# A two-layer transformer block with a state-space block behind it: products read the unscaled residual, and the branch ends work in column quarters

## The reference

```python
def rms_norm(x, g):
    y = xf * lax.rsqrt(jnp.mean(xf * xf, axis=-1, keepdims=True) + EPS)
    return (y * g.astype(jnp.float32)).astype(x.dtype)

for l in range(DEPTH):                       # DEPTH = 2
    xn = rms_norm(h, mix_pre_g[l])
    proj = jnp.einsum('bsd,dc->bsc', xn, w_in[l])      # q, k, v, latents, gates of three mixers
    ...
    h = h + rms_norm(jnp.einsum('bsc,cd->bsd', mix, w_out[l]), mix_post_g[l])
    xa = memory_attention(rms_norm(h, x_pre_g[l]), rms_norm(mem, mem_g[l]), x_wq[l], x_wkv[l], x_wo[l])
    h = h + rms_norm(xa, x_post_g[l])
    ff = swiglu(rms_norm(h, f_pre_g[l]), f_w_gu[l], f_w_down[l])
    h = h + rms_norm(ff, f_post_g[l])
# then second_block: rms_norm, one wide projection, sliding-window attention, an SSM, a GLU
```

## Time and profile before

| | us |
|---|---|
| median of 3 runs (lowest, highest) | 3474.57 (3471.28, 3475.05) |
| span of the profiled execution | 3474.8 |
| PE busy | 3189.5 (92%) |
| DVE busy | 2075.9 (60%) |
| ACT busy | 1525.5 (44%) |
| POOL busy | 166.6 (5%) |

### The profile page before, as it was taken

One profiled execution on the slowest core, in us unless ns is written; L12 is line 12 of the kernel. 1 busy time (PEld: TensorE's weight loads), 2 busy tenths in 40 slices (PEclk: granted clock), 3 DMA queues, 4 the chain that ended last, 5 costly groups with the idle time before them and its releaser, 6 DMA issues.

```text
span 3474.8 us, 48434 instructions
## 1 busy us (share of the span) xinstructions
PE 3189.5 (92%) x17364; PEld 2765.8 (80%) x17364; DVE 2075.9 (60%) x2251; ACT 1525.5 (44%) x1942; POOL 166.6 (5%) x131
## 2 busy tenths in 40 slices
PE   7898897899999997998978999999998977888999
PEld 6798776688888886987866888888876876778997
DVE  5466755555555555577646555555556568987554
ACT  5454544443444344545444443444444443334443
POOL 0000000000000000000000000000001012221000
PEclk9999998899999998999988999999998998889999
DMA  6554453555555554544634555555554333333555
GB/s 235 175 178 165 146 187 109 177 187 188 187 187 189 189 184 134 194 152 140 206 109 154 191 186 190 188 183 191 188 174 136 131 101 107 116 119 129 187 177 176
DMA packets 158218, 577.15 MB, mean 166 GB/s; under 512 B 17409, under 2 KB 20145, under 8 KB 156401
## 3 DMA queue, kind: packets, MB, share of 16 engines
q1 hardware_dynamic: 151120, 549.52, 48.3%
q10 hardware_dynamic: 4800, 13.51, 1.1%
q0 software_dynamic: 2144, 12.02, 1.0%
HBM read 568.43 MB, written 6.55 MB: 165 GB/s over the span
## 4 chain that ended last, share of the span: by engine, by line
PE 76%; DVE 10%; issue 4%; ACT 4%; DVEq 4%; POOL 1%; ACTq 1%; POOLq 0%; DMA 0%
PE acc L600 19%; PE acc L602 19%; PE acc L601 19%; PE acc L608 5%; PE acc L610 5%; PE acc L611 5%; PE tp L619 2%; DVE lo L1359 2%; DVE sr L1880 1%; ACT hi L944 1%; DVEq L1890 1%; POOL small L1962 1%; ACT lg L997 1%; DVE sd L1887 1%; PE tp L900 1%
## 5 line engine op out<-in xcount | busy, mean ns | idle before, releaser
L1359 DVE TENSOR_TENSOR lo<-raw,hi 128x1024 fp32r<-128x1024 f32 x1040 | 1271.8, 1229 | 1017.0 <-ACT hi L944 1008.7
L944 ACT ACTIVATE hi<-raw 128x1024 fp32r<-128x1024 f32 x1040 | 1095.5, 1058 | 1350.0 <-PE acc L602 1005.3
L600 PE MATMUL acc<-hi,xh 128*128 128x512 f32 (+2 forms) x2272 | 883.7, 389 | 0.0
L602 PE MATMUL acc<-hi,xl 128*128 128x512 f32 (+2 forms) x2272 | 876.2, 386 | 0.0
L601 PE MATMUL acc<-lo,xh 128*128 128x512 f32 (+2 forms) x2272 | 876.1, 386 | 0.0
L608 PE MATMUL acc<-xh,hi 128*128 128x256 f32 x1664 | 494.9, 297 | 56.3 <-DVE lo L1359 56.2
L600 PEld LDWEIGHTS acc<-hi,xh 128*128 128x128 f32 x2272 | 429.4, 189 | 85.6 <-issue 1.3
L602 PEld LDWEIGHTS acc<-hi,xl 128*128 128x128 f32 x2272 | 428.8, 189 | 85.1
L601 PEld LDWEIGHTS acc<-lo,xh 128*128 128x128 f32 x2272 | 429.3, 189 | 82.9
L610 PE MATMUL acc<-xl,hi 128*128 128x256 f32 x1664 | 484.1, 291 | 0.0
L611 PE MATMUL acc<-xh,lo 128*128 128x256 f32 x1664 | 483.8, 291 | 0.0
(11 more groups left out here) (347 smaller groups left out, 2832.9 us busy)
## 6 DMA issues: line engine op xcount, KB each, us to landing
raw<-in_stream SPq DMA_DIRECT2D x1040, 512.0 KB, 4.2
gpost<-in_post_g POOLq DMA_DIRECT2D x6, 1024.0 KB, 6.7
bpad<-in_b_pad ACTq DMA_DIRECT2D x8, 512.0 KB, 3.2
row<-in_rows POOLq DMA_DIRECT2D x3, 896.0 KB, 6.1
toep_scratch<-toep ACTq DMA_DIRECT2D x1, 2304.0 KB, 8.1
y<-in_mem SPq DMA_DIRECT2D x1, 2048.0 KB, 8.0
h<-in_x ACTq DMA_DIRECT2D x1, 2048.0 KB, 14.4
mem_scratch<-memkv ACTq DMA_DIRECT2D x1, 2048.0 KB, 6.4
```

What stands on the lines that cost most here:

```text
L600: nc.tensor.matmul(o, ah, hi[s][:, k, 0:g.width], start=first, stop=False)
L602: last = nc.tensor.matmul(o, al, hi[s][:, k, 0:g.width], start=False, stop=final)
L944: nc.scalar.activation(hi[s][:, :, :], raw[s][:, :, :], ACT.Copy).then_inc(hi_done, 1)
L1359: nc.vector.tensor_tensor(lo[s][:, :, :], raw[s][:, :, :], hi[s][:, :, :].bitcast(F32), ALU.subtract).then_inc(split_done, 1)
```

## The change

There are five edits, all in one diff.

1. **Raw norm.** The three norms at the beginning of a layer's branches no longer scale `h`. PE transposes `h` itself as soon as its quarter is there, ACT applies the gain, and the squares and roots of `h` are made later, beside the product. The root is applied where the product is read: by ACT's `scale` for form T groups (`scaled_group`, two instructions of 512 columns for one of 1024), by a broadcast factor on DVE for the form C groups `qk0`, `qk1`, `qk2` and `cu` (PE transposes the broadcast root once in a layer, steps `rs` and `rsb`), inside the exponent for the memory attention, and in the two factors of the feed-forward's gate.
2. **Branch ends in quarters.** For the branches `wo` and `xo`, ACT squares and DVE multiplies by the gain straight from PSUM, each one row half at a time. The sum of the first three quarters is made before the last group is read, POOL adds the last quarter. The addition to `h` is cut into four column quarters (`add_quad`, 128x512, counted by `h_quads`).
3. **The last `down` groups.** DVE adds a group to `y`, waits for ACT's squares of it and multiplies by the gain, all before it goes on to the next units. The last quarter gets its gain in `add_quad(3, True)`.
4. **Split limits.** Before the last group, both engines now split three units of the next branch (before: one on the way, the others after the read).
5. **The layer loop is written out.** `Fori(0, L)` becomes `for layer in range(L)`; the inner loop of the feed-forward stays. The second block keeps the old `norm`, and adds all four quarters ahead of it.

```diff
@@ PE
+            def raw_norm(pos, k, tag, turns):
+                def quad(q):
+                    o = take_turn(pe, pos, turns[f"{tag}{q}"])
+                    for t in range(NT):
+                        pe.wait_ge(h_quads, pos.n(24, 8 * k + 2 * q + t + 1))
+                        for c in range(4):
+                            last = nc.tensor.transpose(o[:, c, t * P:(t + 1) * P],
+                                                       h[:, t, (4 * q + c) * P:(4 * q + c + 1) * P], ident[:, :])
+                    last.then_inc(tp_full, 1)
+                for q in (0, 1):
+                    quad(q)
+                def unit_ready(n):
+                    q = n // 2
+                    if n % 2 == 0:
+                        pe.wait_ge(x_half, pos.n(12, 4 * k + q + 1))
+                    else:
+                        after_turn(pe, pos, turns[f"{tag}{q}"])
+                        if q < 2:
+                            quad(q + 2)
@@ ACT
+            def scaled_group(pos, g, out, func=ACT.Copy):
+                units.ahead(pos, g)
+                a = see_group(act, pos, g)
+                for t in range(NT):
+                    last = nc.scalar.activation(out[:, t, :], a[:, t, 0:g.width], func, scale=rs[:, t:t + 1])
+                last.then_inc(acc_read[g.parity], 1)
-                        hold(act, h_rows, pos.n(6, 2 * branch + t + 1), passed)
+                        hold(act, h_quads, pos.n(24, 8 * branch + 7 + t), passed)
+            def raw_norm(pos, k, tag, turns, gain, g):
+                for q in range(4):
+                    if q:
+                        units.before(pos, g, 2 * q - 2, g.end)
+                    o = see_turn(act, pos, turns[f"{tag}{q}"])
+                    for c in range(4):
+                        last = nc.scalar.activation(xh[:, 4 * q + c, :], o[:, c, :], ACT.Copy, scale=gain(4 * q + c))
+                        if c % 2:
+                            last.then_inc(x_pair, 1)
+                squares_in(pos, h, k)
@@ DVE, branch_out
-                    units.ahead(pos, g, g.end + 1 if n == 3 else LU + SLOTS)
+                    units.ahead(pos, g)
+                    if n == 3:
+                        dve.wait_ge(out_squares, pos.n(12, 4 * k + 3))
+                        nc.vector.tensor_reduce(psum_, pss[:, :, 0:3], AX.X, ALU.add)
...
+                    if not add:
+                        nc.vector.tensor_tensor(part[:, 1, :], a[:, 1, :], row_gain, ALU.mult).then_inc(y_taken, 1)
+                        dve.wait_ge(first_squares, pos.n(8, 4 * k + n + 1))
...
+                    elif n < 3:
+                        nc.vector.tensor_tensor(part, part, a[:, :, :], ALU.add).then_inc(acc_read[g.parity], 1)
+                        dve.wait_ge(out_squares, pos.n(12, 4 * k + n + 1))
+                        nc.vector.tensor_tensor(part, part, gains(n), ALU.mult)
@@ DVE
+            def add_quad(q, add=False):
+                cols = slice(q * W, (q + 1) * W)
+                if q == 3 and add:
+                    nc.vector.tensor_tensor(y[:, :, cols], y[:, :, cols], gains(q), ALU.mult)
+                    dve.drain()
+                for t in range(NT):
+                    nc.vector.scalar_tensor_tensor(h[:, t, cols], y[:, t, cols], prs[:, t:t + 1], h[:, t, cols],
+                                                   ALU.mult, ALU.add).then_inc(h_quads, 1)
+                    elif step == "out" and at[0] in ("qk0", "qk1", "qk2"):
...
+                            last = nc.vector.tensor_tensor(out_, a[:, first:final, :], rsb[:, :].unsqueeze(1)
+                                                           .to_broadcast([P, final - first, T]), ALU.mult)
```

More of the change, by code:

```diff
@@ L661, in _ @@
             product(pos, MG["mem_v1"], xh, xl)
-            with pe.Fori(0, L) as layer:
+            for layer in range(L):
                 pos = Pos(layer)
-                ready = norm(pos, 0, "pre", LTP)
+                ready = raw_norm(pos, 0, "pre", LTP)
                 for step, *at in MIX:
@@ L800, in _ @@
                     after_turn(pe, pos, LTP[f"xV{i}"])
-                for n in range(4):
-                    product(pos, LG[f"xo{n}"], cqh, cql)
-                ready = norm(pos, 2, "fpre", LTP)
+                branch_products(pos, 1, "xo", cqh, cql)
+                ready = raw_norm(pos, 2, "fpre", LTP)
                 def across(pos, j):
@@ L1056, in _ @@
             units.next -= MU
-            with act.Fori(0, L) as layer:
+            for layer in range(L):
                 pos = Pos(layer)
                 hold(act, par_loaded, pos.n(32, 32), passed)
-                norm(pos, 0, "pre", LTP, lambda c: pcol("mix_pre_g", c), h, LG["cq"])
+                raw_norm(pos, 0, "pre", LTP, lambda c: pcol("mix_pre_g", c), LG["cq"])
                 act.wait_ge(lam_ready, pos.n(2, 1))
@@ L1184, in gate @@
                         act.wait_ge(gated, pos.n("gated", j))
-                    nc.scalar.activation(sg[:, :, :], a[:, :, :], ACT.Silu).then_inc(acc_read[g.parity], 1)
+                    else:
+                        act.wait_ge(in_roots, pos.n("norm", 3 * NT))
+                    for t in range(NT):
+                        last = nc.scalar.activation(sg[:, t, :], a[:, t, :], ACT.Silu, scale=rs[:, t:t + 1])
+                    last.then_inc(acc_read[g.parity], 1)
                 def across(pos, j):
@@ new lines, in raw_norm @@
+            def raw_norm(pos, k, tag, turns, gain, g, sums=True, add=False):
+                if sums:
+                    add_quad(0)
+                    add_quad(1)
+                for q in range(4):
+                    o = tp[turns[f"{tag}{q}"] % 2]
+                    for c in range(4):
+                        if c % 2 == 0:
+                            dve.wait_ge(x_pair, pos.n(24, 8 * k + 2 * q + c // 2 + 1))
+                        last = nc.vector.scalar_tensor_tensor(xl[:, 4 * q + c, :], o[:, c, :], gain(4 * q + c),
+                                                              xh[:, 4 * q + c, :].bitcast(F32), ALU.mult, ALU.subtract)
+                        if c == 1:
+                            last.then_inc(x_half, 1)
+                    last.then_inc(tp_read[turns[f"{tag}{q}"] % 2], 1)
+                    if sums and q < 2:
+                        add_quad(q + 2, add)
+                    units.before(pos, g, 2 * q, g.end)
@@ L1735, in _ @@
             dve.wait_ge(par2_loaded, 16)
+            for q in range(4):
+                add_quad(q, True)
+            dve.drain()
             norm(pos, 0, "norm", STP, lambda c: spar[:, SC["norm_w"].start + c:SC["norm_w"].start + c + 1], h,
```

204 lines of the change are left out of this document (132 added, 72 removed).

## The result

The changed kernel took 3399.45 us (3396.21 to 3402.10, 4 runs), the kernel before beside it 3474.81 (3471.28 to 3476.81, 4 runs). The ratio is 0.9786, with a 95% interval of 0.9775 to 0.9798. The gain is 75 us.

A forecast was written before the change was run, and what follows sets the result against it. PE was taken as the bound, three quarters of the chain that ended last. 44.4 + 9.5 + 13.7 - 6.2 - 7.0 = 54.4 us off 3474.8 gave 3420 us, range 3404 to 3442.

The forecast's parts named there:

- The mechanism: Norms `wo` to `xq`, `xo` to `gate0`, both layers: squares, roots, scalings leave the chain; net 11.1 us each, 44.4 together.
- the turn: Norm between the layers: product at T+12.7 instead of T+23.2, a gain of 9.5 us (7 to 12).
- T: End of the last product before a norm; the prediction counts times in us from it.
- rival (b): First units after a norm: DVE becomes the bound, 4 us in each of 5 norms, 3440 us; 9%.
- Rival (a): Behind norms: clock stays low as long as before, to T+23.7; 29 us less gain, 3449 us; 10%.
- (c): Written-out second layer starves the engines of instructions, slower than before, 3490 us; 2%.
- (d): Chain not shortened because `h` is not ready in quarters; only the costs, within 0.2%; 1%.
- the sign of the top keys: Mixing stretch: top-key part longer by 1.4 us, as DVE reads `qk1` in two halves; 2.8 us for two layers.
- POOL does two operations of 0.97 and 0.71 ..., as before.: Four norms: POOL's two operations keep their durations, with 0.24 between, root at T+4.0 instead of T+5.3.
- The clock ... I take 1.5, as before the change.: Products behind the four norms: low clock still costs 1.5 us each, between none and 2.5.
- The second block's norm: Old norm behind the new branch end: loses 6.2 us (-8 to -4), from root 2.7, additions 2.0, squares 1.5 later.
- the price of the mixing stretch: Both layers' mixing: costs of 7.0 us (1 to 15), including split reads of `qk1`, extra DVE work and POOL's loads.

The follow-up runs named there:

- The runs with and without a PSUM operand: Changed kernel plus two DVE operations between a branch's last read and its root wait: 3403.80 us with both operands in SBUF, 3399.00 us with one in PSUM.

## Why the prediction missed

**Right.** The mechanism: idle time before the transposes of `h` 3.8 us three times and 4.2 once (predicted near 4.7), 7.3 at the turn (8.7), none in layer 0, 17.0 before the second block (18.5). Layer 0's product started at T+3.6 (T+3.3). PE has no wait for L1522, and none for `lo` in the first units behind a raw norm: rival (b), DVE as the bound, did not occur. Rival (a) didn't: the low clock ends with the transposes before `gate0`, at T+9.3 and T+8.7 in `xq` and at T+13.1 at the turn, not at T+23.7. Rivals (c) and (d) neither. And the sign of the top keys came: behind the two reads of `qk1` there is a new wait of PE for a split,

```profile
252.64 0.36 PE L624 MATMUL acc<-ckh,hi 128*128 128x256 f32 x1 [1.31 <-DVE lo L1445]
```

which all ten kernels with the new stretch have in both layers, at 1.3 to 1.5 us (predicted 1.4). The waits for splits after it vary without an edit.

**Wrong, 1: "POOL does two operations of 0.97 and 0.71 ..., as before."** I carried a duration over without asking what stood beside it. 0.97 was a wait for DVE's L1387, and that is the instruction which edit 2 moves ahead. The runs with and without a PSUM operand show the cause, and the rows the size: 0.97 - 0.19, 0.8 us a norm. In the four norms PE's idle time is 3.1 us less than my 4 x 4.7, nearly all of it this; at the turn and in the second block it is 0.8 each.

**Wrong, 2: "The clock ... I take 1.5, as before the change."** The two products of `gate0` ran at full clock from their start, as the windows show, and those of `xq` lost 0.7 and 0.9 us. Before, the four had lost 1.5 to 2.0 each, 7.1 together. So the clock gave back 5.6 us where my equal terms before and after gave nothing; the lower end of my term, "at best none", was nearer the truth. That a shorter idle stretch does this is read from the windows; no run changed the clock alone, and the one that lengthened the idle time to 5.5 us still paid only for the idle time. The low clock during the 16 transposes also ended early in some, so they took 3.2 to 3.7 us for 3.9; over the four norms the products started 1.4 us earlier by it.

**Wrong, 3: edit 5 was priced at the turn alone.** I wrote of the turn that a table load and DVE's late start "leave the chain", and of the other places nothing. The loop written out gave 7 us in all, 2.1 of them at the turn; 1.4 at layer 0's beginning, and in the memory attention of both layers 2.1 to 2.3 us each in the profiled executions. The first two stood in my sums, which counted from where the product starts; the last two stood nowhere. The order of instructions showed where the wait stood; I read it only on the engines around the norms.

**Wrong, 4: the second block's norm.** It lost 4.3 us (first product 21.0 us behind the last of layer 1, then 25.3), not 6.2: the last group was read 2.5 us late and not 3.4, and POOL's operation was short here too. That brings the block to -4.3; the 2 us up to the -2.3 of the table lie scattered in its products.

Together, in the four stages that gave 17.3 us more than predicted: 3.1 for the root and POOL, 5.6 for the clock in the products, 1.4 for the transposes, some 4 for the loop in the attention (4.5 in the kernel with the loop alone), 14 in all. The rest is a difference in the feed-forwards: before, a window at 0.75 lay over a wait in the last `down` groups, after it did not. PE and a window before,

```profile
1346.21 0.49 PE L600 MATMUL acc<-hi,hTh 128*128 128x512 f32 x1 [2.54 <-DVE hTl L1695]
```

```profile
1345.00:1350.00 5.00, 3.79 (x11) 3.00 (x12) 2.12 (x2) 0.67 (x1) 0.00 (x0) 0.75 0.33 116
```

and after:

```profile
1307.13 0.50 PE L616 MATMUL acc<-hi,hTh 128*128 128x512 f32 x1 [2.37 <-DVE hTl L1839]
```

```profile
1304.00:1309.00 5.00, 2.63 (x15) 2.07 (x14) 3.50 (x3) 1.97 (x2) 0.00 (x0) 1.00 0.29 105
```

It is worth some 1.7 us a layer, half of the 3.4 that such a stretch lasts, 3.4 in both; with it the sum is 17.5. But the changed kernel and its versions, whose wait is the same 2.37, have the low stretch at 8 of their 20 places and not at the others, and the kernel with the loop alone has it at both with that wait. It is not settled by the edit, and what settles it stays open. So does the price of the mixing stretch beyond the new wait: I predicted 7.0 us. The pair of traces has 2.8 and 6.1 us more of products in the two layers, but the changed stretch took 363.9 to 367.7 and 365.0 to 368.8 us over the kernels here, without an edit in it. Against 365.4 and 363.7 in the mean of the three kernels with the old one, the ten with the new one have 366.5 and 366.9: 4 us, with a scatter as large. Part of the scatter lies in PE's waits for splits at the top keys: 6.1 to 7.8 us in a layer with the old stretch, 5.5 to 9.2 with the new one.

## What to carry to other kernels

A duration read from a trace belongs to its neighbours: before carrying one over, see what it ends with. A small operation that ends, again and again, within a few hundredths of a larger one of another engine is probably a wait; what it costs is gone once the other moves. When a loop is written out, look in the order of instructions at every wait that stood on a register instruction, in front of table loads above all; exchanging two lines can give the same without unrolling, and costs time where the loop is already written out. And where a norm holds PE up, take the work that only the read-out needs (here the squares) off the queues ahead of the first products, before shortening the work that is left.

## What was new of the hardware

- POOL's addition or scaling of 128x2 took 0.19 us alone. Beside a VectorE operation with two SBUF operands, or beside L1367, it ended 0.05 to 0.06 us behind that operation, and so took 0.39 to 1.02; with a PSUM operand in VectorE's operation it took 0.19 again.
- With 3.8 us of idle time the granted clock was still 1.00 during it and 0.58 in the 4.1 us behind it; waits of 5.5 us instead of 3.8 cost no more than the difference.
- The same 2.37 us wait was followed by a stretch at the low clock at 8 of 20 places in the changed kernel and its versions, and at the others not.
- With two waits ahead of an activation, the table load stood behind the one written first in the loop and behind the one written second with constants (behind the maximum at 565.83 and, with the lines exchanged and constants, at 540.85; beside it at 561.84 and 565.35).
- ACT's first ACTIVATE started 0.02 us behind the end of a table load (565.83 + 1.28 = 567.11, then 567.13).
